# Column sums and four-row spreads of the first two mixers, moved from between the weight units to between the tiles of a unit

## What is computed

```python
def even_mixer(h, ...):
    c_q, c_kv, k_pe, qkv, z, a, b = split_last(h @ w_in, ...)
    q = (rms_norm(c_q, q_a_norm) @ w_q_up)...        # needs the sum of squares of c_q by token
    kv = (rms_norm(c_kv, kv_a_norm) @ w_kv_up)...    # and of c_kv
    ...
    qkv = jax.nn.silu(causal_depthwise_conv(qkv, conv_w))
    gq = l2_norm(gq...); gk = l2_norm(gk...)         # sums of squares by token and head
    g = -jnp.exp(a_log) * jax.nn.softplus(a + dt_bias)   # gates, 4 heads
    beta = jax.nn.sigmoid(b)                             # betas, 4 heads
    o_b = gated_delta_chunked(gq, gk, gv, g, beta)
    ...

def odd_mixer(h, ...):
    q, k, v, q_idx, k_idx, w_idx = split_last(h @ w_in, ...)
    q = rms_norm(q.reshape(B, S, 8, 128), q_norm)    # sums of squares by token and head
    ...
```

## Time and profile before

| | us |
|---|---|
| median of 3 runs | 1758.43 |
| lowest, highest run | 1750.75, 1760.58 |
| the profiled execution's own time | 1756.41 |
| its span, first to last instruction | 1754.6 |
| TensorE busy in the span | 1694.4 |
| VectorE busy | 1290.4 |
| ScalarE busy | 997.5 |

### The profile page before, as it was taken

The page is one execution under the profiler, slowest core; times in us unless marked ns, Lnnn a source line. Parts: engine busy times, 40 slices in busy tenths (PEclk is TensorE's granted clock), DMA queues, the critical chain, the costliest instruction groups (busy, mean ns, idle before and its releaser), DMA issues.

```text
span 1754.6 us, 37767 instructions
## 1 busy us (share of the span) xinstructions
PE 1694.4 (97%) x14502; PEld 1571.6 (90%) x14502; DVE 1290.4 (74%) x2137; ACT 997.5 (57%) x1562; POOL 3.0 (0%) x9
## 2 busy tenths in 40 slices
PE   7999999999999999999999999989999999899998
PEld 6999899889999989999988999989999998798887
DVE  6777867658777887777768777877788775566776
ACT  5544655445544564445555544568887885344444
POOL 0000000000000000000000000000000000000000
PEclk9999989899999999999989999999999999999999
DMA  6555543115555456554425655445555550055554
GB/s 228 191 189 186 161 132 109 62 35 177 192 190 190 158 168 191 180 183 165 145 73 174 192 189 191 158 160 188 176 183 185 179 169 4 21 175 174 188 188 144
DMA packets 75865, 278.24 MB, mean 159 GB/s; under 512 B 8433, under 2 KB 8689, under 8 KB 75249
## 3 DMA queue, kind: packets, MB, share of 16 engines
q1 hardware_dynamic: 75168, 273.58, 47.7%
q0 software_dynamic: 592, 3.15, 0.5%
HBM read 274.59 MB, written 2.10 MB: 158 GB/s over the span
## 4 chain that ended last, share of the span: by engine, by line
PE 83%; DVE 8%; ACT 7%; issue 2%; DMA 0%; SPq 0%; DVEq 0%; ACTq 0%
PE ps L475 81%; DVE w_lo L464 2%; ACT w_hi L456 2%; PE ps L2467 1%; DVE rstd L607 1%; DVE x L941 1%; DVE h L568 1%; ACT L2792 0%; ACT L2776 0%; DVE arena L909 0%; DMA x<-x_t 0%; DVE arena L913 0%; ACT h L560 0%; DVE arena L654 0%; DVE arena L602 0%
## 5 line engine op out<-in xcount | busy, mean ns | idle before, releaser
L475 PE MATMUL ps<-h,w_hi 128*128 128x256 f32 (+1 forms) x3380 | 732.7, 307 | 0.0
L464 DVE TENSOR_TENSOR w_lo<-raw,w_hi 128x1024 fp32r<-128x1024 f32 x514 | 621.3, 1215 | 87.7 <-ACT w_hi L456 69.1
L456 ACT ACTIVATE w_hi<-raw 128x1024 fp32r<-128x1024 f32 x514 | 539.4, 1052 | 222.0 <-PE ps L475 200.6
L475 PE MATMUL ps<-h,w_lo 128*128 128x256 f32 x2026 | 582.9, 288 | 21.0 <-DVE w_lo L464 13.8
L475 PEld LDWEIGHTS ps<-h,w_hi 128*128 128x128 f32 x3380 | 552.2, 192 | 28.2
L475 PEld LDWEIGHTS ps<-h,w_lo 128*128 128x128 f32 x2026 | 388.6, 192 | 27.7 <-DVE w_lo L464 12.2
L475 PE MATMUL ps<-h_of_feed_forward,w_hi 128*128 128x512 f32 (+1 forms) x1088 | 351.4, 374 | 0.0
L475 PE MATMUL ps<-h_of_feed_forward,w_lo 128*128 128x256 f32 x1000 | 278.4, 281 | 0.8 <-issue 0.6
L894 ACT ACTIVATE arena<-ps 128x256 f32<-128x256 f32 x208 | 79.7, 385 | 269.3 <-PE ps L475 269.3
L475 PEld LDWEIGHTS ps<-h_of_feed_forward,w_hi 128*128 128x128 f32 x1088 | 198.1, 188 | 36.4
L475 PE MATMUL ps<-a_hi,w_lo 128*128 128x256 f32 x776 | 218.0, 281 | 4.6 <-DVE a_lo L929 4.6
(11 more groups left out here) (354 smaller groups left out, 1449.8 us busy)
## 6 DMA issues: line engine op xcount, KB each, us to landing
raw<-weights SPq DMA_DIRECT2D x514, 512.0 KB, 3.4
con<-shape_constants SPq DMA_DIRECT2D x1, 1618.0 KB, 10.6
x<-x_t SPq DMA_DIRECT2D x1, 1024.0 KB, 5.4
stored<-x POOLq DMA_DIRECT2D x1, 1024.0 KB, 4.8
x<-stored POOLq DMA_DIRECT2D x1, 1024.0 KB, 8.0
out_t<-arena SPq DMA_DIRECT2D x4, 256.0 KB, 2.1
arena<-p_t POOLq DMA_DIRECT2D x2, 256.0 KB, 3.6
arena<-final_gain POOLq DMA_DIRECT2D x1, 512.0 KB, 4.6
```

The source lines that it names most:

```text
L456: A.activation(w_hi[:, u % RING, 0:n], raw[:, u % RING, 0:n], ACT.Copy).then_inc(s_hi, 1)
L464: V.tensor_tensor(w_lo[:, u % RING, 0:n], raw[:, u % RING, 0:n], f(w_hi[:, u % RING, 0:n]), SUB)\
L475: return TE.matmul(o, lhsT, rhs, start=start, stop=stop, skip_group_check=True)
```

## The change

The small matmuls of the five blocks are the same as before, with the same operands and banks. `linear` gets an argument `between_tiles`, a function called after each tile but the last. The block of unit 5 is now spread over the gaps 0 to 4 of unit 6 (4, 6, 6, 4 and 4 records), that of unit 11 over the gaps 0 to 5 of unit 12 (2 records in each of four gaps, then 4 and 4), that of unit 12 over the gaps 0 to 3 of unit 13 (2 each), and that of unit 17 over the gaps 0 to 6 of unit 18 (8, then 4 each). In "odd", the sums of head 0 to 4 stand in gap 3 of units 10 to 14 (4 records each), those of heads 5 and 6 within unit 15, and those of head 7 after it. The semaphore waits move with the matmuls that need them. ScalarE's and VectorE's programs are unchanged.

```diff
-        def linear(pe, u, o, i=None, norm=None, normed=None, src=None):
+        def linear(pe, u, o, i=None, norm=None, normed=None, src=None, between_tiles=None):
...
                 last = wmm(o, u, k, hi[:, k, :], lo[:, k, :], k == 0, k == KT - 1)
+                if between_tiles is not None and k < KT - 1:
+                    between_tiles(k)
             last.then_inc(s_prod, 1)
 
...
-                def rows_of(n):
-
-                    if n == 5:
+                def low_sums(k):
+
+                    if k == 0:
                         sa("low")
                         pe.wait_ge(s_nrm, nrm_at[order["even"]] + 1)
                         for tb in range(NB):
                             last = mm(ps[:, 1, tb:tb + 1], rstd[0:1, blk(tb)], ident[0:1, 0:1])
                         did(last, "rsc")
-                        for r, ks in enumerate(((0, 1, 2), (3, 4))):
-                            for tb in range(NB):
-                                for k in ks:
-                                    last = mm(ps[:, 0, 2 * r + tb:2 * r + tb + 1], sq[:, k, blk(tb)], ones[:, 0:1],
-                                              k == ks[0], k == ks[-1])
-                        did(last, "n1m")
+                    elif k < 5:
+                        r, tb = (k - 1) // 2, (k - 1) % 2
+                        ks = ((0, 1, 2), (3, 4))[r]
+                        for k_ in ks:
+                            last = mm(ps[:, 0, 2 * r + tb:2 * r + tb + 1], sq[:, k_, blk(tb)], ones[:, 0:1],
+                                      k_ == ks[0], k_ == ks[-1])
+                        if k == 4:
+                            did(last, "n1m")
+
+                def gates_spread(k):
+
+                    if k == 0:
+                        va("gc")
+                    if k < 4:
+                        mm(ps[:, 2 + k // 2, k % 2 * T:k % 2 * T + T], sel(k, 0, 4), rr[0:4, :])
+                    elif k == 4:
+                        for c in range(NB):
+                            mm(ps[:, 4, 4 * c:4 * c + 4], rr[0:4, blk(c)], ident[0:4, 0:4])
+                    elif k == 5:
+                        sa("beta")
+                        for c in range(NB):
+                            last = mm(ps[:, 4, 8 + 4 * c:12 + 4 * c], rro[0:4, blk(c)], ident[0:4, 0:4])
+                        did(last, "gbg")
+
+                def betas_spread(k):
+
+                    if k == 0:
+                        va("lown")
+                    if k < 4:
+                        last = mm(ps[:, k // 2, k % 2 * T:k % 2 * T + T], sel(k, 0, 4), rro[0:4, :])
+                        if k == 3:
+                            did(last, "gbb")
+
+                def keys_squared(k):
+
+                    if k == 0:
+                        va("dd")
+                        sa("sqk")
+                    for k_ in ((0, 1) if k == 0 else (k + 1,)):
+                        for tb in range(NB):
+                            last = mm(ps[:, 2, 8 * tb + k_:8 * tb + k_ + 1], sq[:, 5 + k_, blk(tb)], ones[:, 0:1])
+                    if k == 6:
+                        did(last, "n1g")
+                within = {6: low_sums, 12: gates_spread, 13: betas_spread, 18: keys_squared}
+
+                def rows_of(n):
+
                     if n == 7:
...
-                    if n == 11:
-                        va("gc")
...
-                        did(last, "gbg")
-                    if n == 12:
-                        va("lown")
...
-                        did(last, "gbb")
                     if n == 13:
...
-                    if n == 17:
-                        va("dd")
-                        sa("sqk")
...
-                        did(last, "n1g")
                     if n == 19:
...
                     elif n > 1:
                         linear(pe, u0 + n, ps[:, in_bank(n), 0:T], normed=order["even"] if n == 5 else None,
-                               src=h_two if n < 5 else None)
+                               src=h_two if n < 5 else None, between_tiles=within.get(n))
                     rows_of(n)
...
+                def query_sums(hd):
+
+                    sa(f"in{7 + hd}")
+                    if hd == 0:
+                        sa("rl7")
+                    for tb in range(NB):
+                        last = mm(ps[:, 0, 8 * tb + hd:8 * tb + hd + 1], sqq[:, hd, blk(tb)], ones[:, 0:1])
+                    return last
+
...
                     if n == 15:
-                        sa("in14")
-                        sa("rl7")
-                        for tb in range(NB):
-                            for hd in range(8):
-                                last = mm(ps[:, 0, 8 * tb + hd:8 * tb + hd + 1], sqq[:, hd, blk(tb)], ones[:, 0:1])
-                        did(last, "sumq")
+                        did(query_sums(7), "sumq")
                         va("kn")
                         scores(0, (6, 7))
...
                 for n in range(2, 15):
                     if n >= 3:
                         sa(f"in{n - 3}")
-                    linear(pe, u0 + n, ps[:, in_bank(n), 0:T])
+                    linear(pe, u0 + n, ps[:, in_bank(n), 0:T],
+                           between_tiles=None if n < 10 else lambda k: query_sums(n - 10) if k == 3 else None)
                     between(n)
                 for n in (15, 16):
                     if n == 15:
@@ -2034,6 +2060,8 @@
                             c_ = slice(j * T, j * T + T)
                             last = mm3(ps[:, 4 + tb, 0:T], h_hi[:, k, blk(tb)], h_lo[:, k, blk(tb)],
                                        w_hi[:, u % RING, c_], w_lo[:, u % RING, c_], k == 0, k == 7)
+                        if n == 15 and j in (0, 2):
+                            query_sums(5 + j // 2)
                     last.then_inc(s_prod, 1)
                     between(n)
```

More of the change, by code:

```diff
@@ L1166, in rows_of @@
                         did(last, "bc1")
-                    if n == 11:
-                        va("gc")
[L1169 to L1175, removed]
-                        did(last, "gbg")
-                    if n == 12:
-                        va("lown")
-                        for g in range(4):
-                            last = mm(ps[:, g // 2, g % 2 * T:g % 2 * T + T], sel(g, 0, 4), rro[0:4, :])
-                        did(last, "gbb")
                     if n == 13:
@@ L1187, in rows_of @@
                         did(last, "kp")
-                    if n == 17:
-                        va("dd")
-                        sa("sqk")
-                        for tb in range(NB):
-                            for k in range(8):
-                                last = mm(ps[:, 2, 8 * tb + k:8 * tb + k + 1], sq[:, 5 + k, blk(tb)], ones[:, 0:1])
-                        did(last, "n1g")
                     if n == 19:
```

## The result

| | before | after |
|---|---|---|
| median of runs taken side by side (20 each), us | 1757.63 | 1762.36 |
| lowest, highest, us | 1750.75, 1760.58 | 1754.25, 1767.17 |
| the profiled execution's own time, us | 1756.41 | 1763.26 |

The ratio is 1.0025, 95% interval [1.0015, 1.0035]: 4.4 us slower. The forecast was 1754 us with a range of 1745 to 1762; the measured median lies 0.4 us above that range.

What follows compares the result with a forecast made beforehand. TensorE, busy 97% of the span, was taken as the bound, its clock falling after five small-matmul blocks. Terms -3.3 - 3.5 - 1.7 - 0.3 + 0.7 = -8.1 us, halved to -4, gave 1754 us, range 1745 to 1762.

Steps and rivals of the forecast that it cites:

- Units 12 and 13 get 16 and 8 ... I take both as gone, -3.5: Clock term: with their small matmuls spread over gaps, units 12 and 13 lose their clock drops, -3.5 us.
- named 8 as a sign of being wrong: Listed sign of a wrong forecast: a unit 12 of 8 us or more; 5.5 us was expected.
- a mix in which small matmuls take as much time as tiles: Units 6 and 18: no row shows such a mix; unit 6 taken as half of 3.35, -1.7, unit 18 unchanged.
- The third rival: Slower: clock falls inside a diluted unit and stays down to its end; +8.1 us, 1766 us; chance 0.10.
- +0.1 for each of seven new four-row switches: Serial cost of interleaving: +0.1 us per new four-row switch, 0 for the rest, +0.7 us in all.
- the 0.7 a pair: Listed sign of a wrong forecast: four-row pairs that cost over 0.7 us each.
- my bound of +0.10: Upper bound per new switch: time the first four-row record after a big matmul takes beyond a slot.
- The rival of hidden loads: Weight loads pulled ahead of matmuls in flight make isolated small matmuls cheaper, -2.8 us; 1751 us; chance 0.05.
- The halving: The sum of -8.1 us cut to -4, because executions in which fewer blocks fall have less to win.
- no effect on the clock: Rival: blocks do not cause the clock drops, or diluted units trip it as often; 1759 us; chance 0.18.
- "odd", -3.3 forecast: Units 10 to 16 of "odd": the clock drop at unit 15's block, scores(0) and unit 16 goes, -3.27 us.
- cover of 2.7 us: Late spreads in unit 12: unit 14's remainder done at 257.4, needed at 260.1, so the wait costs 0.

Runs made afterwards that it cites:

- gates_only: Kernel before with only units 12 and 13 having their small matmuls between weight tiles, other blocks as before; 1763.04 us, ratio 1.0050, +8.8 us.
- unit12_only: Kernel before with only unit 12's small matmuls between its weight tiles, the rest as blocks; 1759.76 us, ratio 1.0029, +5.1 us.
- one_gap: gates_only, but all four four-row pairs of each unit stand together in its gap 3; 1756.35 us, ratio 1.0001 against the kernel before.
- full_rows: Changed kernel with the eight pairs of units 12 and 13 on 128 rows instead of four; 1748.55 us, ratio 0.9959 against the kernel before.
- no_gates: The change without units 12 and 13, whose small matmuls stay blocks; 1752.85 us, ratio 0.9983 against the kernel before, -3.0 us.
- odd_only: Kernel before with only the change's edits in "odd", all blocks of "even" as before; 1754.18 us, ratio 0.9982, -3.2 us.
- block_full_rows: Kernel before, blocks in place, with the eight spreads after units 11 and 12 on 128 rows instead of four; 1751.35 us, ratio 0.9980, -3.5 us.
- dense_blocks: Kernel before, blocks in place, their small matmuls made 128 rows by 128 columns or more, except two one-row ones; 1746.23 us, ratio 0.9944, -9.8 us.

## Why the prediction was wrong

- **The step that failed** is "Units 12 and 13 get 16 and 8 ... I take both as gone, -3.5". Instead of 3.5 less they took 7.5 more, and the key copies and units 14 to 17 another 2.5. gates_only carries it alone (+8.8), unit12_only shows that unit 12's six gaps start it (+5.1), one_gap that spreading the pairs is what does it (0). In unit12_only unit 12 took over 9 us, where the prediction had 5.5 and named 8 as a sign of being wrong. My argument was that 2.71 us of small matmuls, spread over six gaps of a 2.81 us unit, is thin enough, and no row stood behind it: the only rows of a thin mix are of "odd", with 0.9 us in one block and 0.45 us to come beside 2.81. In the same paragraph I called unit 6, with 24 x 0.111 = 2.67 us, a mix in which small matmuls take as much time as tiles, and left it open. Unit 12's mix is the same, and by my own measure it was as open as unit 6.
- **The third rival** (the clock falls inside a diluted unit and stays down) is what happened in units 12 and 13. It priced their excess over full clock at 4.9 + 4.3 = 9.2 us; measured is 21.28 - (5.62 + 2.71 + 1.92) = 11.0, of which some 2.7 are switches that are dearer at full clock too (next point). It stopped at the unit's end, but the clock stayed low through the key copies and most of unit 14, worth 2.5 us more. Units 6 and 18 did not follow it: unit 6 fell in one of the three profiles that have its thin sums between tiles (after; not in full_rows and no_gates) and came out even, unit 18 in one (full_rows, for 10.2 us; not in after, where it won 1.5, and not in no_gates). So the share of small matmuls does not settle by itself whether a unit falls. A chance of 0.10 was too low for a case that no row excluded.
- **The term that was mis-sized**: +0.1 for each of seven new four-row switches. A pair costs 1.17 - 0.35 = 0.82 us between tiles and 1.92 / 4 = 0.48 in the block: +0.34 each, 2.7 for eight, and over the 0.7 a pair that I had named as a sign of being wrong. Beside this my bound of +0.10 from the first record of a block was no bound, since it held one switch and not the way back. The rival of hidden loads had the sign wrong: a pair between tiles costs more, not less.
- **The halving** of -8.1 to -4, for executions in which fewer blocks fall, has no support in the parts that worked: odd_only wins 3.2 of 3.3, block_full_rows 3.5 of 3.5 and dense_blocks 9.8 of 11.8. Without it the forecast would have been 1750, farther off. That the measured 1762.36 lies only 0.4 us above the range is no credit to the reasoning either, since the range's upper part stood for no effect on the clock and for the slower rival.
- **Right**: "odd", -3.3 forecast, -3.20 in the trace, -3.2 in odd_only; unit 15 to 16 with the added records 11.03 us against 10.96; the exponentials 3.2 us earlier. One-column records cost the same between tiles (20 for 2.24 us). Unit 18 starts without the 0.35 us wait. TensorE did not wait for unit 14's remainder, but the forecast's cover of 2.7 us was read wrong by about 1: it let VectorE's differences start with the end of the spreads, and they stand behind ScalarE's exponentials (before, the block ended at 251.62 and the differences started at 252.92). In after the remainder is done at 264.8 and unit 14 starts at 274.5, with units 12 and 13 as long as they were.
- **The clock as the lever** was right in size: all five falls were priced at 11.8 us, and dense_blocks, which has none of them and moves nothing, gains 9.8 [7.2, 12.5]; some 0.5 of it are blocks that got shorter at the same clock (2.54 and 1.54 us against 2.71 and 1.92). block_full_rows wins for units 12 and 13 the 3.5 that I had written down for the change.
- **The reading of the cause** was half right. Busy without a gap, "but on matmuls of one or four columns, or of four rows", named the right thing, and I then reasoned about spreading it out when the record could be filled up. The Trainium skill, "TensorE: Matmul & The Clock Gate", section "Why this matters for your kernels", ties mid-kernel drops to stretches in which TensorE is idle. The two blocks of 3.56 us, both with a matmul record open all the time and with different clocks behind them, do not agree with it for this kernel, as far as "busy" is read by open records; how much of a one-column record the array works is in no trace here, so what exactly the clock answers to stays open.

## What to carry to other kernels

When TensorE is the bound and its granted clock dips behind a block of small matmuls, first make those matmuls as dense as the array (128 rows, 128 columns), where a record costs no more for it; here that gave 0.56% and no reordering. Thinning them out between real tiles helps where the small part is small (0.45 us beside 2.81); where it is as large as the tiles the clock can fall inside the unit, as it did in unit 12 (with four-row pairs) in three profiles of three and in units 6 and 18 in one of three each, and it can then stay down longer than behind a block. Why it stays down so long is not shown. When a forecast leans on "spread thin enough", write down the ratio of small to large time in the row that vouches for it and in the place it is used on.

## What the runs showed of the hardware that I had not expected

- A matmul of four rows between two of 128 pays at both switches. The timelines of weight loads show it, here of after:

```profile
251.61 0.29 PEld L475 LDWEIGHTS ps<-arena,con 4*128 4x128 f32 x2
252.23 0.19 PEld L475 LDWEIGHTS ps<-h,w_lo 128*128 128x128 f32 x1 [0.33 <-issue]
```

and here of full_rows:

```profile
247.34 0.30 PEld L475 LDWEIGHTS ps<-arena,con 128*128 128x128 f32 x2
247.67 0.19 PEld L475 LDWEIGHTS ps<-h,w_lo 128*128 128x128 f32 x1
```

  With four rows the load begins only with its matmul (both at 251.61), and so does the tile's behind it (252.23, after 0.33 us without a load). With 128 rows it begins 0.11 us before its matmul (247.34, 247.45), and the tile's 0.02 us before (247.67, 247.69). That a load is not taken ahead across a change of rows is what these rows show; why is open.
- The lower clock lasted 23.9, 20.5 and 13.7 us in the three profiled executions (after, gates_only, unit12_only) that had unit 12 diluted by four-row pairs, and went on through tiles with nothing between them: most of unit 14 in the first two, all of unit 13 in the third. No fall behind a block in "even" from 220 to 290 us of the kernel before was longer than 6.8.
- A record of 128 columns costs what one of a single column costs (32 in 3.56 us either way), and eight records of 256 columns in a block cost less with 128 rows (1.54 us, dense_blocks) than with four (1.92).
